# Spreading the delta-rule gate rows of a hybrid backbone by one bf16 product of three exact parts

## The chip, the cores and the metric

The kernel runs on 1 core of one Trainium2 chip. The metric is the time of one execution in device microseconds, as the median of several runs. Engines are named as in the profile: PE is TensorE (PEld its weight loads), DVE is VectorE, ACT is ScalarE, POOL is GpSimd, SP is SyncE, which issues most DMAs.

## The reference

A two-layer latent backbone with 256 latent tokens and 256 context tokens of width 1024. Layer 0 mixes by gated linear attention and Mamba-2, layer 1 by a conformer convolution and a bidirectional gated delta rule; a mixture of 16 experts follows each. The change touches the gates of the delta rule in layer 1 alone:

```
ga, gb, q, k, v, og, a_raw, b_raw = split_cols(h @ w_in + b_in, CD_SPLITS)
beta = sigmoid(b_raw)                                   # 2 directions x 8 heads
logg = -exp(gdn_a_log) * softplus(a_raw + gdn_dt_bias)  # 2 directions x 8 heads
# per chunk of 64 tokens and head:
gc = cumsum(logg)
decay = exp(where(tril, gc[:, None] - gc[None, :], -inf))
m = eye + where(strict, (k * beta) @ k.T * decay, 0)
u, w = solve(m, [v * beta, k * beta * exp(gc)])
aqk = (q @ k.T) * decay;   qg = q * exp(gc);   kd = k * exp(glast - gc)
```

So each head and direction needs its row of cumulative logs `gc` once along the partitions (a column per token) and once along the free axis, in every partition (a "spread" row), to form the differences of `decay`. The backward direction runs over the reversed sequence.

## The kernel before

Everything lives in SBUF, tokens on the free axis (T = 512: context first, then latent) or on 128 partitions in 4 tiles. The program is written out by hand for five engines; each works its queue in order and the order around the change is that of the code, tied by named semaphores.

**Projection of layer 1** (`project`, PE L804, ACT L1705, DVE L2273). The 49 column tiles of the input projection run over j. PE does the tile's 8 products (L820) and, two tiles behind, `turn` (L764), which transposes the convolved tile j-2. A q, k or v tile goes: PE tile j, ACT copy out of the bank (L1717), DVE's three-tap convolution at j (`convolve`, L2267, L2269, L2271), ACT's Silu (L1648), PE's `turn` in step j+2, DVE's copy out of the bank (`turned`, L2256). `turn` number m waits for its Silu and for the copy of turn m-2. Between these DVE runs the conformer's 31 taps a tile (L2280) and, at the end of a step j, a piece of the gate work (`gate_softplus(j)`, DVE L2315, ACT L1740).

**Gates.** Projection tile 0 ("small") holds the gate rows: the a columns (for the logs) of the two directions on partitions 0 to 7 and 32 to 39, the b columns (for beta) on 64 and 96 upward. DVE adds the bias at j = 2 (L2339), works out the softplus at j = 8 and 14 (L2715 to L2729), multiplies by -exp(a_log) (L2346), and at j = 16 takes the two cumulative sums (L2349, L2350) into `gcb`, which is the tile `small`. At j = 20 it lays the last values of each chunk on diagonals (`albuf2`, L2358). PE turns `gcb` to tokens-on-partitions and adds up `albuf2` at j = 24 (`gdn_gates`, L991, L992). DVE copies these out at j = 25 (L2323 to L2328), and PE waits for that before a modulation product at j = 28 (L627).

**The delta-rule scan** (`gdn`, PE L994, ACT L1769, DVE L2377, POOL L3088). Ten rounds `it` = -1 to 8; in a round head n = it+1 is prepared, head p = it is solved by six levels of block products (`level_r` L1013, `level_p` L1036) and head s = it-1 runs its state recurrence (`new_values` L1115, `state_step` L1127, `state_out` L1146). `spread(n, d)` (L1053) makes the spread row of head n and direction d: a column of the fp32 identity, broadcast to 128 columns, times `gcb` (128x512). There are 16 of them: d = 0 stands between `level_r(p, 1)` and `level_p(p, 1)`, d = 1 between `level_p(p, 1)` and `level_r(p, 2)`. ACT's `decay` (L1804 Abs, L1805 and L1807 Exp) reads the bank.

Of the kernel before, what the change touches and what calls it, by code (L numbers as in the profile page):

```python
# [12 lines left out]
P = 128  # L13
# [128 lines left out]
def hybrid_backbone(nc, A, out):  # L142
    rg = Ring()
    assert tuple(rg.place[rg.first[f"moe{layer}"]] % RING for layer in range(2)) == MOE_SLOT
    with ExitStack() as ctx:
# [112 lines left out]
        with ExitStack() as st:  # L258
# [6 lines left out]
            gts = sb("gts", [P, 7, NT, 2, 8], F32, st)  # L265
            alogx = sb("alogx", [P, 1], F32, st)
            rkq = sb("rkq", [P, KD, 6], F32, st)
# [13 lines left out]
            gcb = small[:, :]  # L281
            albuf2 = gts[:, 0:4, :, :, :].rearrange("p i t d h -> p i (t d h)")
            gcT, sT, negc, ekd, egl2, skT, ngcT = [gts[:, i, :, :, :] for i in range(7)]
# [318 lines left out]
        def _(pe):  # L602
# [384 lines left out]
            def gdn_gates():  # L987
                pe.wait_ge(sg("gate_cums"), 2)
                pe.wait_ge(sg("mod_added"), 5)
                for t in range(NT):  # L990
                    nc.tensor.transpose(ps[7][:, t * P:(t + 1) * P], gcb[:, t * P:(t + 1) * P], ident[:, :])  # L991
                mm(ps[6][:, 0:256], ones[:, :], albuf2, start=True, stop=True).then_inc(sg("gate_cums_turned"), 1)  # L992

            def gdn():  # L994
# [49 lines left out]
                def spread(n, d):  # L1044

                    if n >= KD:
                        return
                    if n > 0:
                        if d == 0:
                            pe.wait_ge(sg("gdn_S"), 2 * n)  # L1050
                        else:
                            pe.wait_ge(sg("gdn_aqk"), n)
                    mm(ps[4 + d], ident[:, n + 32 * d:n + 32 * d + 1].broadcast_to([P, P]), gcb,  # L1053
                       start=True, stop=True).then_inc(sg("gdn_spr"), 1)
# [519 lines left out]
        def _(act):  # L1574
# [165 lines left out]
            def gate_softplus(j):  # L1740
# [15 lines left out]
                if j == 1:  # L1756
                    act.drain()
                    A_(small[64:128, :], small[64:128, :], ACT.Sigmoid)
                if j == 3:
                    A_(small[64:128, :], small[64:128, :], ACT.Sqrt)  # L1760
                if j == 6:
                    act.wait_ge(sg("sp_abs"), 2)
                    A_(alogx[0:64, :], cols[0:64, COL_AT["gdn_alog"]:COL_AT["gdn_alog"] + 1], ACT.Exp)
                    A_(g_u[0:64, :], g_u[0:64, :], ACT.Exp, scale=-1.0).then_inc(sg("sp_u"), 1)
                if j == 12:
                    act.wait_ge(sg("sp_w"), 2)
                    A_(g_l[0:64, :], g_w[0:64, :], ACT.Ln).then_inc(sg("sp_ln"), 1)

# [338 lines left out]
        def _(dve):  # L2107
# [207 lines left out]
            def gate_softplus(j):  # L2315

                rows = slice(0, 64)
                if j - 2 in CD_HALVES and CD_HALVES[j - 2][1] == 1:
                    modulation(1, CD_HALVES[j - 2][0])
                if j == 25:  # L2320
                    dve.wait_ge(sg("gate_cums_turned"), 2)
                    tm = ps[7].rearrange("p (t d r) -> p t d r", t=NT, d=4)
                    V.tensor_copy(gcT, tm[:, :, 0:2, 0:8])  # L2323
                    V.tensor_scalar(ngcT, tm[:, :, 0:2, 0:8], -1.0, None, ALU.mult)
                    V.tensor_copy(sT, tm[:, :, 2:4, 0:8])
                    V.tensor_copy(egl2, ps[6][:, 0:256].rearrange("p (t d r) -> p t d r", t=NT, d=2)[:, :, :, 0:8])
                    dve.drain()
# [6 lines left out]
                if j == 45:  # L2334
                    key_scales(slice(0, 6), 4)
                    dve.drain().then_inc(sg("conf_ready"), 1)
                if j == 2:
                    dve.wait_ge(sg("proj_evacuated"), PLAN["cd"][0]["no"] + 1)
                    V.tensor_scalar(g_z[rows], small[rows, :], cols[rows, COL_AT["gdn_dtb"]:COL_AT["gdn_dtb"] + 1], None, ALU.add)  # L2339
# [4 lines left out]
                if j == 14:  # L2344
                    softplus_end(rows, g_z, g_u, g_l, g_sp)
                    V.tensor_scalar(small[rows, :], g_sp[rows], alogx[rows, :], -1.0, ALU.mult, ALU.mult)  # L2346
                if j == 16:
                    dve.drain()
                    V.tensor_tensor_scan(gcb[0:32, :], rst128[0:32, :], small[0:32, :], 0.0, ALU.mult, ALU.add)  # L2349
                    V.tensor_tensor_scan(gcb[32:64, ::-1], rst128[32:64, :], small[32:64, ::-1], 0.0, ALU.mult, ALU.add)  # L2350
                if j == 20:
# [3 lines left out]
                    for t in range(NT):  # L2355
                        for d in range(2):
                            e = t * P + edge(d)
                            last = V.tensor_scalar(albuf2[0:64, t, 32 * d:32 * d + 32], ident[0:64, 32 * d:32 * d + 32], gcb[0:64, e:e + 1], None, ALU.mult)  # L2358
                    last.then_inc(sg("gate_cums"), 1)
# [817 lines left out]
def pack_columns(np, a):  # L3177
# [31 lines left out]
    for d in range(2):  # L3209
        got[64 + 32 * d:80 + 32 * d, COL_AT["ssd_dtb"]] = a["ssd_dt_bias"][0, d]  # L3210
        got[64 + 32 * d:80 + 32 * d, COL_AT["ssd_alog"]] = a["ssd_a_log"][0, d]
        got[32 * d:32 * d + 8, COL_AT["gdn_dtb"]] = a["gdn_dt_bias"][0, d]
        got[32 * d:32 * d + 8, COL_AT["gdn_alog"]] = a["gdn_a_log"][0, d]
    b = a["cd_b_in"][0]
# [17 lines left out]
CD_PLACE = {"ga": 0, "gb": 1024, "q": 2048, "k": 3072, "v": 4096, "og": 5120}  # L3232
CD_SMALL = [(0, 6144, 8), (32, 6152, 8), (64, 6160, 8), (96, 6168, 8)]

# [69 lines left out]
```

## Time and profile before

| | |
|---|---|
| median of 3 runs | 2189.32 us (2188.63 to 2191.02) |
| span of the profiled execution | 2185.7 us; its time is not listed apart from the three runs', and the span is 3.6 us under their median |
| PE / DVE / ACT / POOL busy | 1882.4 / 804.4 / 507.6 / 335.2 us |
| projection of layer 1 | about 1142 to 1406 us of the span |
| delta-rule scan | about 1406 to 1661 us |
| output projection and second expert stage | 1661 us to the end; DMA engines 92% busy |
| the 16 spreads (L1053) | 32 PE records of 593 ns (an fp32 product leaves two records) |

Times in a timeline are microseconds from the span's start. "Busy" of PE is the time in which any product is in its pipeline, so neighbouring products overlap. Idle before an instruction stands in square brackets with what ended it. In the chain of waits a row is the part of an instruction that lies on the chain of work that ended last.

### The profile page before, as it was taken

Reading aid. Unit: us, or ns where it says so; the run is one execution under the profiler, and the core shown is the slowest. Engines: PE = TensorE matmul, PEld = TensorE weight load, DVE = VectorE, ACT = ScalarE, POOL = GpSimd, SP = SyncE. Lnnn points to the kernel's source line nnn. Section 1 sums busy time; section 2 is a strip of 40 time slices with the busy share of each in tenths; the row PEclk is TensorE's granted clock in tenths of the full one; section 3 lists DMA queues with packets and bytes.
Section 4 is the critical chain, followed back from the end, with each engine's and each line's share of the span. In section 5 each row is a group of like instructions: output and inputs, shape, how many; then the busy total and the mean of one; then the engine's idle time right before and its main releaser. Section 6 shows DMA issues by size and latency. Waiting matters only on the chain.

```text
span 2185.7 us, 32921 instructions
## 1 busy us (share of the span) xinstructions
PE 1882.4 (86%) x14024; PEld 1132.1 (52%) x14024; DVE 804.4 (37%) x1427; ACT 507.6 (23%) x1119; POOL 335.2 (15%) x323
## 2 busy tenths in 40 slices
PE   6999889999999998888889999989999975666565
PEld 3874668745875433333236556677787731212112
DVE  3331757555633010000026877566774300000001
ACT  2452321343012100001023323444442100000001
POOL 1431054322320000000013000054540000000000
PEclk9999999999999999999999999999999998878888
DMA  9321031240239999999993433200004699999997
GB/s 385 142 86 73 5 118 78 119 190 1 89 150 384 428 430 426 429 431 431 428 407 147 169 154 140 103 2 2 2 2 174 233 428 429 430 427 432 430 430 298
DMA packets 46689, 528.07 MB, mean 242 GB/s; under 512 B 3408, under 2 KB 7760, under 8 KB 23120
## 3 DMA queue, kind: packets, MB, share of 16 engines
q1 hardware_dynamic: 44784, 522.56, 57.3%
q10 hardware_dynamic: 1760, 3.42, 0.4%
q8 instruction: 111, 1.82, 0.3%
q14 instruction: 34, 0.28, 0.0%
HBM read 524.91 MB, written 1.05 MB: 241 GB/s over the span
## 4 chain that ended last, share of the span: by engine, by line
PE 53%; DMA 28%; DVE 12%; issue 2%; ACT 2%; DVEq 1%; PEld 1%; PEldq 0%; POOLq 0%; POOL 0%; ACTq 0%; SPq 0%
DMA ring<-in_moe_w 27%; PE bank L1435 12%; PE bank L709 8%; PE bank L820 7%; PE bank L1317 4%; PE bank L1250 3%; PE bank L788 3%; DVE ring L2421 2%; DVE x L2280 2%; PE bank L1036 2%; PE bank L1013 2%; DVE x L2859 1%; PE bank L961 1%; DMA ring<-in_mod_w 1%; PE bank L627 1%
## 5 line engine op out<-in xcount | busy, mean ns | idle before, releaser
L1435 PE MATMUL bank<-ring,xgs 128*32 128x512 f32 x2984 | 374.0, 655 | 129.4 <-DMA ring<-in_moe_w 128.0
L1435 PEld LDWEIGHTS bank<-ring,xgs 128*32 128x32 f32 x2984 | 106.3, 119 | 370.6 <-issue 284.9
L1435 PE MATMUL bank<-ring,hT 128*32 128x512 f32 x1488 | 190.1, 663 | 75.3 <-DMA ring<-in_moe_w 75.1
L820 PE MATMUL bank<-hT,ring 128*128 128x256 f32 (+1 forms) x784 | 232.7, 454 | 2.0 <-ACT hT L1607 1.4
L2700 DVE SCALAR_TENSOR_TENSOR x<-bank,modT,x 128x256 f32<-128x256 f32 x96 | 42.4, 480 | 457.1 <-PE bank L1461 456.9
L820 PEld LDWEIGHTS bank<-hT,ring 128*128 128x128 f32 x784 | 146.6, 190 | 82.3 <-issue 66.8
L1435 PEld LDWEIGHTS bank<-ring,hT 128*32 128x32 f32 x1488 | 52.3, 120 | 199.3 <-issue 152.6
L2280 DVE SCALAR_TENSOR_TENSOR x<-gluR,cols,x 128x256 f32<-128x256 f32 x240 | 116.2, 484 | 16.6 <-issue 0.9
L709 PE MATMUL bank<-hT,ring 128*128 128x256 f32 x432 | 99.9, 381 | 3.7 <-ACT ssd_g L1658 2.2
L709 PEld LDWEIGHTS bank<-hT,ring 128*128 128x128 f32 x432 | 81.1, 190 | 17.9 <-issue 6.2
L3091 POOL MEMSET gluR<- 128x3008 f32 x1 | 2.6, 2610 | 498.9 <-DVEq L2710 498.9
L2689 DVE TENSOR_TENSOR hT<-mrow,bank 128x512 f32<-128x512 f32 x16 | 11.0, 685 | 170.8 <-PE bank L1435 170.8
L2689 DVE TENSOR_TENSOR hT<-small,bank 128x512 f32<-128x512 f32 x8 | 5.5, 688 | 174.4 <-PE bank L1435 174.4
L3108 POOL TENSOR_TENSOR ring<-ring,pmask 128x512 f32<-128x512 f32 x40 | 51.0, 1274 | 77.8 <-DVE ring L2409 68.6
L1923 ACT ACTIVATE xgs<-bank 128x512 f32<-128x512 f32 x24 | 14.3, 597 | 197.0 <-PE bank L1392 197.0
L709 PE MATMUL bank<-g_v,ring 128*128 128x256 f32 x256 | 58.4, 381 | 0.0
L788 PE MATMUL bank<-ring,hT 128*128 128x512 f32 x128 | 55.2, 593 | 0.3 <-issue 0.3
L2961 POOL TENSOR_TENSOR ring<-ring 128x512 f32<-128x512 f32 x18 | 31.2, 1734 | 155.4 <-PE bank L709 155.4
L1392 PEld LDWEIGHTS bank<-pick,htok 128*128 128x128 f32 x384 | 44.5, 191 | 18.4 <-issue 17.2
L709 PEld LDWEIGHTS bank<-g_v,ring 128*128 128x128 f32 x256 | 47.9, 190 | 11.3 <-issue 4.0
L627 PE MATMUL bank<-ring,act_c 128*32 128x512 f32 x384 | 46.8, 635 | 7.6 <-DMA ring<-in_mod_w 5.3
L1933 ACT ACTIVATE mrow<-bank 128x512 f32<-128x512 f32 x16 | 9.5, 594 | 186.9 <-PE bank L1435 186.9
(573 smaller groups left out, 3026.0 us busy)
## 6 DMA issues: line engine op xcount, KB each, us to landing
ring<-in_moe_w SPq DMA_DIRECT2D x56, 4096.0 KB, 22.8
ring<-in_moe_w SPq DMA_DIRECT2D x28, 2048.0 KB, 21.1
ring<-in_moe_w SPq DMA_DIRECT2D x55, 1024.0 KB, 14.4
ring<-in_mod_w SPq DMA_DIRECT2D x12, 4096.0 KB, 13.4
ring<-in_moe_w SPq DMA_DIRECT2D x12, 3072.0 KB, 22.0
ring<-in_cd_w SPq DMA_DIRECT2D x6, 4096.0 KB, 14.1
ring<-in_ab_w SPq DMA_DIRECT2D x5, 4096.0 KB, 15.3
ring<-in_ab_wo SPq DMA_DIRECT2D x2, 4096.0 KB, 14.9
```

Source lines behind the costliest of these rows:

```text
L627: last = mm(ps[6][32 * g:32 * g + 32, :], act_c[:, 4 * kh + k, :], w[:, g, k, :], start=(kh == 0 and k == 0), stop=(kh == 1 and k == 3), t ...
L709: last = mm(to, w[:, k0 + k, :], right(k), start=(start and k == 0), stop=(k == 3), skip_group_check=True)
L788: last = mm(ps[n % 4].rearrange("p (e c) -> p e c", c=P), hT[:, k, t * P:t * P + P], w[:, e0:e0 + 4, k, :], start=(k == 0), stop=(k == KD ...
L820: last = mm(ps[p["no"] % 4][:, p["c0"]:T], w[:, k, :], hT[:, k, p["c0"]:T], start=(k == 0), stop=(k == KD - 1))
L1013: last = mm(U4[r, d ^ hf, t, :], S[r, d, t, r], H[r, d ^ hf, t, :], start=True, stop=True, skip_group_check=True, tile_position=(64 * hf, ...
L1036: last = mm(P4[r, v, t, :], H[r, v, t, :], Rs[r, v, t, :], start=True, stop=True, skip_group_check=True, tile_position=(64 * hf, 64 * hf))
L1250: last = mm(ps[c % 4][:, SEQ:T], w[:, k, :], conf[:, k, :] if k < 8 else og[:, k - 8, :], start=(k == 0), stop=(k == 15))
L1317: last = mm(out_banks(v)[bank], w[:, k0 + k, :], right[k], start=(start and k == 0), stop=(k == 7), skip_group_check=True)
L1392: last = mm(ps[(4, 7)[b % 2]][:, k * P:(k + 1) * P], htok[:, 2 * s + tt, ch:ch + P], pick[:, s, tt, P * q:P * q + P], start=(tt == 0), sto ...
L1435: last = mm(ps[banks + s][32 * j:32 * j + 32, :], lhs[s][:, 4 * kh + k, 32 * j:32 * j + 32], piece(g, k, j), start=(kh == 0 and k == 0), s ...
L2280: V.scalar_tensor_tensor(y, gluR[:, i, :, w:w + GW], col("conf_w", 8 * w + i), y, ALU.mult, ALU.add)
L3108: G.tensor_tensor(Hb[(l + 1) % 3], Fb[p % 2], pmask[:, l - 1, :].unsqueeze(1).unsqueeze(1).broadcast_to([P, 2, NT, 64]), ALU.mult).then_in ...
```

## The change

The a columns of the small tile are laid out three times: packed as 16 rows (direction, head) on partitions 0 to 15, 32 to 47 and 64 to 79, and the b columns on 96 to 111. All gate steps up to the logs run over 96 partitions instead of 64 (same number of columns). Each of the 96 rows gets both cumulative sums, of which a 0 or 1 column for its direction (`sides2`) has cleared the wrong one, and their sum is `gcb`. At j = 18 the fp32 row is cut into three bf16 parts, one in each group of partitions (`gcs`, in the storage of `rst128`), whose sum is the fp32 value. `pickb2` is a bf16 tile with three ones a column, so that one bf16 product picks a row and adds its three parts. `albuf2` shrinks from 64 to 16 columns a tile, and its product from 256 to 64 columns.

```
             gts = sb("gts", [P, 7, NT, 2, 8], F32, st)
-            alogx = sb("alogx", [P, 1], F32, st)
+            steps2 = sb("steps2", [P, 3], F32, st)
+            alogx, sides2 = steps2[:, 0:1], steps2[:, 1:3]
+            pickb2 = sb("pickb2", [P, 16], BF16, st)
...
-            albuf2 = gts[:, 0:4, :, :, :].rearrange("p i t d h -> p i (t d h)")
+            albuf2 = gts[:, 0, :, :, :].rearrange("p t d h -> p t (d h)")
+            gcs = rst128[:, :].bitcast(BF16)[:, 0:T]
...
-                mm(ps[6][:, 0:256], ones[:, :], albuf2, start=True, stop=True).then_inc(sg("gate_cums_turned"), 1)
+                mm(ps[6][:, 0:16 * NT], ones[:, :], albuf2, start=True, stop=True).then_inc(sg("gate_cums_turned"), 1)
...
-                    mm(ps[4 + d], ident[:, n + 32 * d:n + 32 * d + 1].broadcast_to([P, P]), gcb,
+                    mm(ps[4 + d], pickb2[:, 8 * d + n:8 * d + n + 1].broadcast_to([P, P]), gcs,
                        start=True, stop=True).then_inc(sg("gdn_spr"), 1)
...
-                    A_(small[64:128, :], small[64:128, :], ACT.Sigmoid)
+                    A_(small[96:128, :], small[96:128, :], ACT.Sigmoid)
...
-                rows = slice(0, 64)
+                rows = slice(0, 96)
...
                 if j == 2:
+                    V.tensor_tensor(pickb2[:, :], ident[:, 0:16], ident[:, 32:48], ALU.add)
+                    dve.drain()
+                    V.tensor_tensor(pickb2[:, :], pickb2[:, :], ident[:, 64:80], ALU.add)
+                    dve.drain()
+                    V.tensor_reduce(sides2, pickb2[:, :].rearrange("p (d h) -> p d h", d=2), AX.X, ALU.add)
                     dve.wait_ge(sg("proj_evacuated"), PLAN["cd"][0]["no"] + 1)
...
                     softplus_end(rows, g_z, g_u, g_l, g_sp)
-                    V.tensor_scalar(small[rows, :], g_sp[rows], alogx[rows, :], -1.0, ALU.mult, ALU.mult)
+                    V.tensor_scalar(sides2[rows, :], sides2[rows, :], alogx[rows, :], -1.0, ALU.mult, ALU.mult)
+                    dve.drain()
+                    V.tensor_scalar(g_w[rows], g_sp[rows], sides2[rows, 0:1], None, ALU.mult)
+                    V.tensor_scalar(g_l[rows], g_sp[rows], sides2[rows, 1:2], None, ALU.mult)
                 if j == 16:
                     dve.drain()
-                    V.tensor_tensor_scan(gcb[0:32, :], rst128[0:32, :], small[0:32, :], 0.0, ALU.mult, ALU.add)
-                    V.tensor_tensor_scan(gcb[32:64, ::-1], rst128[32:64, :], small[32:64, ::-1], 0.0, ALU.mult, ALU.add)
+                    V.tensor_tensor_scan(g_u[rows], rst128[rows, :], g_w[rows], 0.0, ALU.mult, ALU.add)
+                    V.tensor_tensor_scan(g_z[rows, ::-1], rst128[rows, :], g_l[rows, ::-1], 0.0, ALU.mult, ALU.add)
+                    dve.drain()
+                    V.tensor_tensor(gcb[rows, :], g_u[rows], g_z[rows], ALU.add)
+                if j == 18:
+                    dve.drain()
+                    V.tensor_copy(gcs, gcb)
+                    dve.drain()
+                    V.tensor_tensor(g_w[32:64, :], gcb[32:64, :], gcs[32:64, :], ALU.subtract)
+                    V.tensor_tensor(g_w[64:96, :], gcb[64:96, :], gcs[64:96, :], ALU.subtract)
+                    dve.drain()
+                    V.tensor_copy(gcs[32:64, :], g_w[32:64, :])
+                    V.tensor_copy(gcs[64:96, :], g_w[64:96, :])
+                    dve.drain()
+                    V.tensor_tensor(gcs[64:96, :], g_w[64:96, :], gcs[64:96, :], ALU.subtract)
                 if j == 20:
...
-                            last = V.tensor_scalar(albuf2[0:64, t, 32 * d:32 * d + 32], ident[0:64, 32 * d:32 * d + 32], gcb[0:64, e:e + 1], None, ALU.mult)
+                            last = V.tensor_scalar(albuf2[0:32, t, 8 * d:8 * d + 8], ident[0:32, 8 * d:8 * d + 8], gcb[0:32, e:e + 1], None, ALU.mult)
...
-CD_SMALL = [(0, 6144, 8), (32, 6152, 8), (64, 6160, 8), (96, 6168, 8)]
+CD_SMALL = [(32 * q + 8 * d, 6144 + 8 * d, 8) for q in range(3) for d in range(2)] + [(96, 6160, 8), (104, 6168, 8)]
```

The order of PE, ACT, POOL and SP stays as it was; only names and shapes of their rows change. DVE's queue gets twelve rows more, all in the projection of layer 1. The first place is step j = 2, DVE's queue before the change:

```order
L2280 SCALAR_TENSOR_TENSOR x<-gluR,cols,x 128x256 x6
L2339 TENSOR_SCALAR k_t<-small,cols 64x512
L2341 SCALAR_TENSOR_TENSOR v_t<-k_t 64x512
L2280 SCALAR_TENSOR_TENSOR x<-gluR,cols,x 128x256 x6
L2293 TENSOR_TENSOR gluR<-rstd,rst 128x4x64
```

and of the changed kernel, whose line numbers are a few higher:

```order
L2283 SCALAR_TENSOR_TENSOR x<-gluR,cols,x 128x256 x6
L2341 TENSOR_TENSOR pickb<-ident 128x16
L2343 TENSOR_TENSOR pickb<-pickb,ident 128x16
L2345 TENSOR_REDUCE steps<-pickb 128x2
L2347 TENSOR_SCALAR k_t<-small,cols 96x512
L2349 SCALAR_TENSOR_TENSOR v_t<-k_t 96x512
L2283 SCALAR_TENSOR_TENSOR x<-gluR,cols,x 128x256 x6
```

Three small instructions now stand ahead of the bias. The second place is the end of step 18 and the convolution of tile 19 in DVE's queue (a q tile, 256 columns), before:

```order
L2280 SCALAR_TENSOR_TENSOR x<-gluR,cols,x 128x256 x6
L2267 TENSOR_SCALAR wk<-wk,cols 128x256
L2269 SCALAR_TENSOR_TENSOR wk<-wk,cols 128x256
L2271 SCALAR_TENSOR_TENSOR wk<-wk,cols 128x256
L2256 COPY k_t<-bank 128x512
```

and of the change:

```order
L2283 SCALAR_TENSOR_TENSOR x<-gluR,cols,x 128x256 x6
L2366 CAST rst<-small 128x512
L2368 TENSOR_TENSOR q_t<-small,rst 32x512
L2369 TENSOR_TENSOR q_t<-small,rst 32x512
L2371 CAST rst<-q_t 32x512
L2372 CAST rst<-q_t 32x512
L2374 TENSOR_TENSOR rst<-q_t,rst 32x512
L2270 TENSOR_SCALAR wk<-wk,cols 128x256
L2272 SCALAR_TENSOR_TENSOR wk<-wk,cols 128x256
L2274 SCALAR_TENSOR_TENSOR wk<-wk,cols 128x256
L2259 COPY k_t<-bank 128x512
```

Six instructions stand ahead of the convolution of tile 19 and of the copy that frees a bank. The third place is DVE's end of step 16 (ahead of the convolution of tile 17), of the change:

```order
L2360 SCALAR_TENSOR_TENSOR v_t<-rst,q_t 96x512
L2361 SCALAR_TENSOR_TENSOR k_t<-rst,v_t 96x512
L2363 TENSOR_TENSOR small<-v_t,k_t 96x512
L2270 TENSOR_SCALAR wk<-wk,cols 128x512
L2272 SCALAR_TENSOR_TENSOR wk<-wk,cols 128x512
```

where the third row is new behind the two cumulative sums.

## Rows read from the trace of the kernel before

**Rows 1.** Two stages: length, busy PE, PEld, DVE, ACT, POOL; clock, DMA share, GB/s.
```profile
1158.00:1226.00 68.00, 64.20 (x254) 40.76 (x252) 58.42 (x114) 23.82 (x42) 10.38 (x32) 1.00 0.32 124
...
1406.00:1661.00 255.00, 234.20 (x3672) 198.91 (x3671) 169.39 (x287) 116.91 (x305) 113.53 (x88) 0.99 0.03 13
```

**Rows 2.** Timeline of PE in the projection: start, length, instruction, idle before and releaser.
```profile
1226.36 0.41 PE L764 MATMUL bank<-ident,wk 128*128 128x128 f32 x2 [0.72 <-DVE k_t L2256]
...
1259.78 0.38 PE L764 MATMUL bank<-ident,wk 128*128 128x128 f32 x2
...
1270.75 0.63 PE L991 MATMUL bank<-ident,small 128*128 128x128 f32 x4 [0.26 <-issue]
...
1291.28 3.64 PE L627 MATMUL bank<-ring,act_c 128*32 128x512 f32 x32 [1.15 <-DVE gts L2328]
```

**Rows 3.** Timeline of DVE in the projection.
```profile
1225.53 0.68 DVE L2256 COPY k_t<-bank 128x512 f32<-128x512 f32 x1
...
1234.28 0.68 DVE L2729 SCALAR_TENSOR_TENSOR k_t<-k_t 64x512 f32<-64x512 f32 x1
1235.04 0.48 DVE L2346 TENSOR_SCALAR small<-k_t,alogx 64x512 f32<-64x512 f32 x1
...
1248.72 0.49 DVE L2267 TENSOR_SCALAR wk<-wk,cols 128x512 f32<-128x512 f32 x1 [0.37 <-ACTq L1719]
...
1255.62 0.68 DVE L2256 COPY k_t<-bank 128x512 f32<-128x512 f32 x1
...
1264.27 1.25 DVE L2358 TENSOR_SCALAR gts<-ident,small 64x32 f32<-64x32 f32 x8
...
1271.28 0.49 DVE L2267 TENSOR_SCALAR wk<-wk,cols 128x512 f32<-128x512 f32 x1 [1.21 <-ACTq L1719]
...
1279.47 0.49 DVE L2267 TENSOR_SCALAR wk<-wk,cols 128x512 f32<-128x512 f32 x1 [2.49 <-ACTq L1719]
```

**Rows 4.** DVE's groups by shape: count, busy us, mean ns, idle before.
```profile
L2721 DVE TENSOR_TENSOR k_t<-k_t,v_t 64x512 f32<-64x512 f32 x1 | 0.7, 684 | 0.1
L2715 DVE TENSOR_SCALAR q_t<-v_t 64x512 f32<-64x512 f32 x1 | 0.4, 419 | 0.1
L2369 DVE TENSOR_TENSOR gts<-gts,rkq 128x16 f32<-128x16 f32 x1 | 0.2, 170 | 0.0
```

**Rows 5.** The spreads of line 1053, and the bf16 products of layer 0.
```profile
L1053 PE MATMUL bank<-small,ident x32: 592/593/721, 1406.9 to 1593.6; 128*128 128x512 f32 x32
```
```profile
L921 PE MATMUL bank<-m_far,identb 128*128 128x512 bf16 x32 | 9.7, 384 | 0.0
```

**Rows 6.** The chain of waits, at step 24 and at the scan's start.
```profile
1271.38 0.43 PE bank L992 x2
...
1406.91 1.14 PE bank L1053 x2
```

**Rows 7.** The chain of waits in the round of head 3.
```profile
1504.36 1.68 DVE ring L2421
...
1508.54 0.65 DVE ring L2409
```

**Rows 8.** Timeline of ACT at the scan's start and of PE in head 3's round.
```profile
1408.14 1.14 ACT L1804 ACTIVATE gluR<-bank,gts 128x128 f32<-128x128 f32 x4 [2.41 <-PE bank L1053]
...
1504.49 1.02 PE L1053 MATMUL bank<-small,ident 128*128 128x512 f32 x2
1505.44 1.15 PE L1036 MATMUL bank<-ring 64*64 64x64 f32 x32
...
1509.23 1.15 PE L1013 MATMUL bank<-ring,hT 64*64 64x64 f32 x32 [1.14 <-DVE ring L2409]
```

**Rows 9.** Three stretches of the scan, columns as in the first group.
```profile
1439.00:1443.00 4.00, 2.46 (x52) 2.05 (x46) 3.40 (x4) 0.65 (x2) 1.77 (x2) 1.00 0.00 2
1443.00:1447.00 4.00, 3.73 (x38) 3.12 (x38) 3.92 (x4) 2.04 (x3) 3.08 (x3) 0.57 0.00 0
1505.00:1509.00 4.00, 3.09 (x40) 1.75 (x38) 3.97 (x6) 2.36 (x8) 1.71 (x2) 1.00 0.02 4
```

**Rows 10.** The block product of line 1013 at the lowered clock.
```profile
1443.27 1.98 PE L1013 MATMUL bank<-ring,hT 64*64 64x64 f32 x32 [0.28 <-DVE ring L2421]
```

More of the change, by code:

```diff
@@ L1757, in gate_softplus @@
                     act.drain()
-                    A_(small[64:128, :], small[64:128, :], ACT.Sigmoid)
+                    A_(small[96:128, :], small[96:128, :], ACT.Sigmoid)
                 if j == 3:
-                    A_(small[64:128, :], small[64:128, :], ACT.Sqrt)
+                    A_(small[96:128, :], small[96:128, :], ACT.Sqrt)
                 if j == 6:
                     act.wait_ge(sg("sp_abs"), 2)
-                    A_(alogx[0:64, :], cols[0:64, COL_AT["gdn_alog"]:COL_AT["gdn_alog"] + 1], ACT.Exp)
-                    A_(g_u[0:64, :], g_u[0:64, :], ACT.Exp, scale=-1.0).then_inc(sg("sp_u"), 1)
+                    A_(alogx[0:96, :], cols[0:96, COL_AT["gdn_alog"]:COL_AT["gdn_alog"] + 1], ACT.Exp)
+                    A_(g_u[0:96, :], g_u[0:96, :], ACT.Exp, scale=-1.0).then_inc(sg("sp_u"), 1)
                 if j == 12:
                     act.wait_ge(sg("sp_w"), 2)
-                    A_(g_l[0:64, :], g_w[0:64, :], ACT.Ln).then_inc(sg("sp_ln"), 1)
+                    A_(g_l[0:96, :], g_w[0:96, :], ACT.Ln).then_inc(sg("sp_ln"), 1)
             def gdn():
@@ L2321, in gate_softplus @@
                     dve.wait_ge(sg("gate_cums_turned"), 2)
[L2322 to L2326, printed above, removed]
+                    tm = ps[7].rearrange("p (t d r) -> p t d r", t=NT, d=16)
+                    V.tensor_copy(gcT, tm[:, :, 0:2, :])
+                    V.tensor_scalar(ngcT, tm[:, :, 0:2, :], -1.0, None, ALU.mult)
+                    V.tensor_copy(sT, tm[:, :, 12:14, :])
+                    V.tensor_copy(egl2, ps[6][:, 0:16 * NT].rearrange("p (t d r) -> p t d r", t=NT, d=2))
                     dve.drain()
@@ L3211, in pack_columns @@
         got[64 + 32 * d:80 + 32 * d, COL_AT["ssd_alog"]] = a["ssd_a_log"][0, d]
-        got[32 * d:32 * d + 8, COL_AT["gdn_dtb"]] = a["gdn_dt_bias"][0, d]
-        got[32 * d:32 * d + 8, COL_AT["gdn_alog"]] = a["gdn_a_log"][0, d]
+        for q in range(3):
+            got[32 * q + 8 * d:32 * q + 8 * d + 8, COL_AT["gdn_dtb"]] = a["gdn_dt_bias"][0, d]
+            got[32 * q + 8 * d:32 * q + 8 * d + 8, COL_AT["gdn_alog"]] = a["gdn_a_log"][0, d]
     b = a["cd_b_in"][0]
```

## The prediction

> **What bounds the kernel now.** I read the time by stages first, then the chain of waits stage by stage, then the timelines around each line that the change touches. The change has two places. Most of its DVE work falls into the projection of layer 1, its 16 cheaper products into the scan. In both stages PE is busy nearly all the time, 64.2 of 68 us and 234.2 of 255 us [rows 1], and in both DVE, busy for less, is what PE waits for at the few places where it waits. In the projection DVE starts late, works without a pause from 1158 us, and PE waits for it at the turn of tile 13 (0.72 us at 1226.36) and for the gate columns at 1291.28 (1.15 us) [rows 2]. Between these PE goes at its own pace, and what DVE gains or loses there is seen only at the turns. In the scan each head's round has a part in which DVE is on the chain, from first_level (L2421) to the masked copy at 1508.54 [rows 7], and a part in which PE is. The spreads stand in DVE's part.
>
> **The spreads, removed cost.** A spread is now two fp32 records of 593 ns [rows 5], together 1.02 us from the first's start to the second's end [rows 8]. The bf16 products of layer 0 with the same 512 columns leave one record of 384 ns [rows 5]. So each spread gets shorter by 1.02 - 0.38 = 0.64 us, and 16 of them by 10.2 us of PE time. Where is that on the path? In the round of head 3, the first spread runs at 1504.49, level_p behind it ends at 1505.44 + 1.15 = 1506.59 [rows 8], and DVE takes that product only at about 1508.5, when it has finished its own row of work [rows 7]. That is 1.9 us of slack for level_p before the change. Behind the second spread PE sits idle for 1.14 us until DVE's copy lets L1013 start at 1509.23 [rows 8]. Both savings end in waits for DVE, and the chain of waits has no L1053 in this round. ACT's decay begins 0.64 us earlier and then waits for the same level 2. The other rounds have the same pattern, and the two odd ones (first heads) are bound there by DVE's copies or by ACT's tables. I take nothing for 15 spreads. The first spread is different: it is on the chain for 1.14 us [rows 6], and ACT has waited 2.41 us for it when it starts at 1408.14 [rows 8]. With one record of 0.38 us in the place of 1.14 us this saves 0.76 us, and the second spread of that head is not waited for, since ACT is busy with the first. Bounds: 0.5 to 1.0 us saved there, and 0 to 15 x 0.64 = 9.6 us more if the slack isn't real (a rival below).
>
> **The product of line 992.** It shrinks from 256 to 64 columns; of its 0.43 us on the chain [rows 6] a quarter stays, so 0.3 us less of PE, in a stretch in which PE is the bound.
>
> **DVE's added work, by step.** Instructions behind a drain start 0.08 us after the one before has ended (1234.28 + 0.68 to 1235.04) [rows 3].
> - j = 2: two TENSOR_TENSOR of 128x16 and a small reduce. The row of that shape is 170 ns [rows 4]; with the drains 3 x 0.25 = 0.75 us. Bounds 0.4 to 1.1.
> - j = 14: a 96x2 multiply, 0.25 us, and two scaled copies for one; the one took 0.48 [rows 3], the second adds 0.40. Together 0.65 us. Bounds 0.4 to 0.9.
> - j = 16: the sums cost by columns, not by partitions, so only the added TENSOR_TENSOR counts: 0.68 [rows 4] + 0.08 = 0.76 us. More partitions cost nothing at j = 2, 8 and 14 for the same reason: a TENSOR_SCALAR of 64x512 takes 0.48 and of 128x512 0.49 [rows 3].
> - j = 18: three TENSOR_TENSOR of 512 columns, 3 x 0.68 [rows 4] = 2.04, and three casts to bf16. No cast is in the trace. A one-source instruction from SBUF to SBUF takes 0.42 [rows 4], a copy out of PSUM 0.68 [rows 3]; I take 0.42, since source and target lie in SBUF as there. With 1.26 for the casts and about 0.24 for the drains less the overlap of undrained neighbours, 3.54 us. Bounds 2.4 (casts at half) to 4.6 (casts and joins slower).
> - j = 20: eight multiplies of 8 columns for 32, up to 0.5 us less of 1.25 [rows 3], and a smaller memset. I take 0.3 less.
>
> For the casts the Trainium skill (VectorE: DVE Perf Modes, the perf-mode tier table) says that one-source instructions with both ends in SBUF move two fp32 elements a cycle, and that two-source ones and PSUM operands in fp32 drop to one. The trace agrees: 419 ns against 684 and 683 ns for 512 columns [rows 3, 4]. By the rule a cast is like the 0.42; by the copy's row the three casts would cost 0.8 us more and the sum below would end at 2191.0.
>
> **What hides it.** I follow DVE's lag against the rows of before. Behind j = 2, 14 and 16 it is 0.75 + 0.65 + 0.76 = 2.16 us. The convolution of tile 18 waited 0.37 us for ACT at 1248.72 [rows 3], so 1.8 us remain. Steps 17 and 18 of PE have their Silu more than that ahead. Then comes j = 18, straight in front of the convolution of tile 19: the lag is 1.8 + 3.54 = 5.33 us. The turn of tile 19 needs that convolution, its Silu and the copy of turn 17, which ended at 1255.62 + 0.68 = 1256.30; with the 0.15 us that lay between such a copy's end (1225.53 + 0.68) and the product at 1226.36, PE could have started at 1256.45 and did so at 1259.78 [rows 2, 3]. Slack 3.33 us. So **PE waits and ends up 5.33 - 3.33 = 2.0 us late**. The 0.75 us from j = 2 show first, at the turns up to 1226.36, and are part of these 2.0.
>
> Is more lost later? At the gates' turn (1270.75 before [rows 2]) PE comes at 1272.8; DVE's diagonals, ended at 1265.5, end at about 1270.5. No wait. At tile 23 DVE had waited 1.21 us and at tile 24 2.49 us for ACT [rows 3]. Lag 5.0 at tile 23 becomes 5.0 - 1.21 = 3.8, less 2.49 leaves 1.3, while PE and ACT are 2.0 - 0.3 = 1.7 us late. So from tile 24 DVE waits for ACT again, with some 0.4 us to spare, and the wait for the gate columns at 1291.28 stays 1.15 us. Everything behind, with the scan and the experts' weight stream that starts on its last output, is shifted by the same amount.
>
> **Sum.** +2.0 (turn of tile 19) - 0.3 (L992) - 0.76 (first spread) = +0.9 us. The span goes from 2185.7 to 2186.6. The span lies 3.6 us under the median of 2189.32; with this unchanged, **2190.2 us**. With all bounds on DVE's work low, the cost is 0.1 instead of 2.0; with all high (lag 2.9 - 0.37 + 4.6 = 7.1), 3.8. So the likeliest case runs from 2188.0 to 2192.3.
>
> **Rivals.**
> - *The spreads are on the path after all (faster).* If in each round PE's or ACT's time around the spreads counted, 15 x 0.64 = 9.6 us would come on top: 2180.6 us. For it: PE is busy 92% of the scan [rows 1]. Against it: the chain of each full round passes from L2421 by DVE to L1013, and PE idles right behind the second spread [rows 7, 8].
> - *TensorE's clock falls in the scan (slower).* The products taken away also kept PE busy. In the first head's round a stretch of 4 us with PE busy for 2.46 was followed by 4 us at a granted clock of 0.57, between its levels of 1.2 and 2.4 GHz [rows 9], and the block product then took 1.98 us instead of 1.15 [rows 8, 10]. In the round of head 3, 1505 to 1509 us had PE busy 3.09 us at full clock [rows 9]; without the 1.28 us of two spreads it is 1.8, less than what went ahead of the fall. Right behind stands PE's part of the round, so a fall costs in full: about two such blocks, 2 x 0.83 = 1.7 us a round, over 7 rounds 11.6 us, 2201.8 us. If it happens in half of the rounds, 2196. It decides over 0.2% from three falls on. Against it: 1505 to 1509 lost 0.91 us of PE to idling already, and the clock stood; the one fall came in the one round where the block products also had pauses between them.
> - *DVE's small instructions and drains cost twice as much (slower).* The lag at tile 24 isn't absorbed, and the wait at 1291.28 grows beside the one at 1259.78: lag 8 us gives +4.7 at the turn of tile 19, 2193 to 2194.
> - *The bf16 product isn't shorter.* Then only the 0.76 us are missing, 2191.0. The layer-0 rows speak against it; it is inside the likeliest case.
>
> On the clock the Trainium skill (TensorE: Matmul & The Clock Gate, on the failure mode of PSUM-queue cycling) reports a kernel with short idles between groups of matmuls whose clock swings between both levels. That speaks against this change, as the second rival has it; the trace before shows one such swing in the scan and none in the rounds behind.
>
> **Chances.** Likeliest case 0.70, spreads on the path 0.09, the clock 0.15, DVE twice as dear 0.06. A measurement of this kernel tells about 0.2%, 4.4 us, from no change. Faster by more: 0.09 and 0.01 from noise in the likeliest, 0.10. Slower by more: 0.13 of the clock's 0.15 and 0.04 of DVE's 0.06, 0.17. Within: 0.73. The range takes the likeliest case whole and half of the clock's and most of DVE's: 2186 to 2196.5.
>
> **What would show it.** L1053 with 16 records of about 384 ns. PE idle ahead of the turn of tile 19 by about 1.2 to 2 us, released by DVE, and 1.15 us still ahead of the product at j = 28. Casts of 0.42 us. In the scan rounds as long as before, with PE idle ahead of L1013 at about 1.8 us instead of 1.14, and first ACT decay 1.2 - 0.76 = 0.5 us behind the spread's start. The forecast is wrong if the round gets shorter (first rival), or if the granted clock leaves 1.0 in rounds where it was 1.0 (second).

## The result: 6 us slower, and the profile after

| | before | changed |
|---|---|---|
| median of 8 runs each | 2188.98 us (2187.64 to 2193.13) | 2195.15 us (2192.88 to 2200.08) |
| span of the profiled execution | 2185.7 us | 2192.2 us (that execution: 2193.93 us) |

The ratio is 1.0028 (95% interval 1.0019 to 1.0036): slower by 0.28%, 6.2 us, inside the stated range but above the likeliest case, which ended at 2192.3. In the experiments below, one of the 12 runs of experiment 9 took 3216.04 us at a granted clock of 0.56 over the whole execution, and its ratio leaves this run out. The page of the changed kernel shows no more work than was counted; PE, DVE and ACT are busy for about as long as before. Its clock line, in tenths, reads 9 over the scan's slices as before; the change is too short-lived for it:

```profile
span 2192.2 us, 32909 instructions
PE 1885.1 (86%) x14008; PEld 1135.1 (52%) x14008; DVE 809.4 (37%) x1439; ACT 507.1 (23%) x1119; POOL 335.2 (15%) x323
PEclk9999999999999999999999999999999997878888
```

The two stages that the change touches, changed kernel (columns as in [rows 1]):

```profile
1158.00:1226.00 68.00, 63.38 (x250) 40.06 (x249) 58.49 (x116) 23.88 (x42) 9.87 (x30) 1.00 0.32 124
1406.00:1661.00 255.00, 226.99 (x3626) 197.73 (x3625) 167.09 (x278) 115.73 (x302) 113.91 (x90) 0.96 0.04 14
```

In the scan's window the granted clock is 0.96 where it was 0.99 [rows 1].

**The projection** did what the sum said. PE's timeline of the changed kernel:

```profile
1226.24 0.41 PE L767 MATMUL bank<-ident,wk 128*128 128x128 f32 x2 [0.73 <-DVE k_t L2259]
...
1260.55 0.41 PE L767 MATMUL bank<-ident,wk 128*128 128x128 f32 x2 [0.73 <-DVE k_t L2259]
1271.55 0.63 PE L994 MATMUL bank<-ident,small 128*128 128x128 f32 x4 [0.26 <-issue]
1291.87 3.64 PE L630 MATMUL bank<-ring,act_c 128*32 128x512 f32 x32 [1.15 <-DVE gts L2331]
```

The second row is the turn of tile 19. It had no wait before [rows 2] and now waits for DVE's copy, 0.73 us, on top of what earlier turns passed on. At 1291.87 the wait is 1.15 us as before. DVE's timeline has the instructions that cause it:

```profile
1161.68 0.17 DVE L2341 TENSOR_TENSOR pickb<-ident 128x16 bf16<-128x16 f32 x1
1161.93 0.17 DVE L2343 TENSOR_TENSOR pickb<-pickb,ident 128x16 bf16<-128x16 bf16 x1
1162.18 0.17 DVE L2345 TENSOR_REDUCE steps<-pickb 128x2 f32<-128x16 bf16 x1
1162.27 0.54 DVE L2347 TENSOR_SCALAR k_t<-small,cols 96x512 f32<-96x512 f32 x1
...
1254.76 0.43 DVE L2366 CAST rst<-small 128x512 bf16<-128x512 f32 x1
1255.26 0.68 DVE L2368 TENSOR_TENSOR q_t<-small,rst 32x512 f32<-32x512 f32 x1
...
1258.33 0.35 DVE L2270 TENSOR_SCALAR wk<-wk,cols 128x256 f32<-128x256 f32 x1
...
1280.06 0.49 DVE L2270 TENSOR_SCALAR wk<-wk,cols 128x512 f32<-128x512 f32 x1 [0.33 <-ACTq L1722]
```

The split takes 1258.33 - 1254.76 = 3.6 us, and at tile 24 DVE waits for ACT again (0.33 us left of 2.49 [rows 3]).

**The spread** is one record, 389 ns at the median, and the first ACT decay waits 1.68 us where it waited 2.41 [rows 8]:

```profile
L1056 PE MATMUL bank<-rst,pickb x16: 379/389/634, 1407.5 to 1596.7; 128*128 128x512 bf16 x16
```
```profile
1408.00 1.14 ACT L1807 ACTIVATE gluR<-bank,gts 128x128 f32<-128x128 f32 x4 [1.68 <-PE bank L1056]
```

**The scan's rounds** are where the rest went. PE's timeline in head 3's round:

```profile
1507.83 0.39 PE L1056 MATMUL bank<-rst,pickb 128*128 128x512 bf16 x1 [0.23 <-DVE gluR L2463]
1510.24 1.54 PE L1016 MATMUL bank<-ring,hT 64*64 64x64 f32 x32 [2.02 <-DVE ring L2433]
1511.71 1.22 PE L1149 MATMUL bank<-ring,hT 128*128 128x128 f32 x4
1512.86 1.75 PE L1039 MATMUL bank<-ring 64*64 64x64 f32 x32
```

PE is idle for 0.23 us ahead of the second spread, where it did not wait before, and for 2.02 us ahead of the level's products instead of 1.14 [rows 8], and then these products are slow: 1.54 and 1.75 us in place of 1.15. The windows of the same kernel give the granted clock (last three columns: clock, DMA share, GB/s):

```profile
1442.00:1454.00 12.00, 9.80 (x126) 7.99 (x125) 9.90 (x12) 7.04 (x15) 6.56 (x6) 0.57 0.00 1
1506.00:1510.00 4.00, 1.99 (x37) 1.43 (x33) 3.97 (x6) 2.26 (x8) 1.72 (x2) 1.00 0.02 6
1510.00:1516.00 6.00, 5.76 (x88) 5.18 (x90) 4.38 (x9) 3.15 (x9) 2.46 (x2) 0.72 0.00 0
1540.00:1546.00 6.00, 5.69 (x86) 5.12 (x88) 4.46 (x9) 3.15 (x9) 2.56 (x3) 0.72 0.01 3
1598.00:1604.00 6.00, 4.91 (x73) 4.50 (x74) 4.37 (x9) 2.53 (x7) 2.45 (x2) 0.72 0.01 3
```

A stretch with the clock at its lower level is called a fall from here on. The first lasts some 10 us of 1442 to 1454 (a mean of 0.57 of a clock that is either 1.0 or 0.5); three more of some 3.4 us each stand right behind the idle time of three rounds, in the windows from 1510, 1540 and 1598. The second window is the part of head 3's round that 1505 to 1509 was before, since this round starts 1.0 us later. PE is busy for 1.99 us of its 4, where it was for 3.09 [rows 9]; the forecast's second rival had 1.8. But neither this nor the idle time decides alone: the round of head 5 has as much of both and no fall.

```profile
1566.15:1570.15 4.00, 1.98 (x37) 1.43 (x33) 3.97 (x6) 2.25 (x8) 1.73 (x2) 1.00 0.01 4
```
```profile
1570.39 1.15 PE L1016 MATMUL bank<-ring,hT 64*64 64x64 f32 x32 [2.03 <-DVE ring L2433]
```

The chain of waits carries the slow products of head 3's round in full:

```profile
1509.48 0.72 DVE ring L2433
1510.24 1.54 PE bank L1016 x32
1511.78 1.15 PE bank L1149 x4
1512.93 1.68 PE bank L1039 x32
```

A balance by landmarks that both timelines have (first tile of the projection; last turn; first product of L1086; each round's start of L1017; first product of L1250; end). The round of head n is the one in which head n is solved; it holds the two spreads of head n+1, and head 7's holds none:

| stretch | before | changed | difference |
|---|---|---|---|
| start to first tile of the projection | 1142.52 | 1141.69 | -0.8 (nothing changed there) |
| projection, first tile to last turn | 262.65 | 264.08 | +1.4 |
| last turn to first product of L1086 | 9.96 | 9.22 | -0.7 |
| first product of L1086 to the first round | 25.24 | 25.23 | 0 |
| first round (head 1) | 30.37 | 31.50 | +1.1 |
| the six that follow (heads 2 to 7) | 29.07, 28.69 x4, 26.12 | 29.08, 30.08, 30.08, 28.70, 30.07, 26.11 | +4.2 |
| last round | 22.67 | 22.68 | 0 |
| output projection and experts | 522.35 | 523.68 | +1.3 |

Of the six rounds the three with a fall (heads 3, 4 and 6) are 1.38 to 1.39 us longer each, and the others are as before. Scan together: +4.6 us.

### The profile page after: what moved, and what is told of

Read it like the earlier page. It is cut to its first block, busy times and chain, and to the rows that moved or that the text cites. A ratio compares the mean times of both kernels' runs of the same rounds, so it can differ in the third digit from the quotient of the medians.

```text
span 2192.2 us, 32909 instructions
## 1 busy us (share of the span) xinstructions
PE 1885.1 (86%) x14008; PEld 1135.1 (52%) x14008; DVE 809.4 (37%) x1439; ACT 507.1 (23%) x1119; POOL 335.2 (15%) x323
## 4 chain that ended last, share of the span: by engine, by line
PE 52%; DMA 27%; DVE 13%; issue 2%; ACT 2%; DVEq 2%; PEld 0%; PEldq 0%; POOLq 0%; POOL 0%; ACTq 0%; SPq 0%
DMA ring<-in_moe_w 26%; PE bank L1438 13%; PE bank L712 8%; PE bank L823 6%; PE bank L1320 3%; PE bank L1253 3%; PE bank L791 3%; DVE x L2283 2%; DVE ring L2445 2%; PE bank L1039 2%; PE bank L1016 2%; DMA ring<-in_mod_w 1%; DVE x L2883 1%; PE bank L964 1%; PE bank L1395 1%
## 5 line engine op out<-in xcount | busy, mean ns | idle before, releaser
L1438 PE MATMUL bank<-ring,hT 128*32 128x512 f32 x1488 | 195.0, 678 | 69.3 <-DMA ring<-in_moe_w 69.3
```

Source lines behind the costliest of these rows:

```text
L1438: last = mm(ps[banks + s][32 * j:32 * j + 32, :], lhs[s][:, 4 * kh + k, 32 * j:32 * j + 32], piece(g, k, j), start=(kh == 0 and k == 0), s ...
```

## Experiments

The theory after the first look (clock theory): the products taken away had kept TensorE's clock up; it now falls right behind the idle time in front of a PE-bound stretch. The rival: DVE's new work, or something it shifts, costs all of it. In each experiment the ratio is against the kernel before, run beside it on the same chip: 2190.03 us for experiments 1 to 4, 2188.88 for 5 to 7, 2190.03 for 8 and 9, on three chips. Windows and rounds are read from one profiled execution of each version. An idle product is one whose result nobody uses. "Rounds" means the start-to-start times of line 1017's product as in the table.

**1. Only the spread's product undone.**

```
-mm(ps[4 + d], pickb2[:, 8 * d + n:8 * d + n + 1].broadcast_to([P, P]), gcs,
+mm(ps[4 + d], ident[:, n + 8 * d:n + 8 * d + 1].broadcast_to([P, P]), gcb,
```

> The changed kernel with the 16 spreads made by the fp32 product again (a column of the fp32 identity times the fp32 rows); all of DVE's new work stays, and nobody uses the bf16 parts. Clock theory (TensorE's clock falls in the scan because the shorter spreads leave it idle for longer): the granted clock leaves 1.0 in the scan once, as in the kernel before, the falls at heads 3, 4 and 6 (1.4 us each) are gone, only the 1.4 us of the projection stay: about 1.4 us over before, 2190.4. Rival (DVE's new work costs the rest, somewhere behind the projection): as the changed kernel, about 6 us over before, 2195. Noise rival (the 6 us are a slow expert stage): anything between, with the scan as long as in the changed kernel's trace.

Measured 2190.99 us (2188.27 to 2193.35), before 2190.03; ratio 1.0005 (0.9996 to 1.0014). The projection takes 264.07 us, as in the changed kernel, and rounds 30.36, 29.08, 28.70, 28.71, 28.72, 28.73, 26.10 us, as before. The windows of the places of the falls:

```profile
1442.00:1454.00 12.00, 7.26 (x138) 5.85 (x139) 9.88 (x11) 5.66 (x15) 5.79 (x4) 1.00 0.01 1
1512.00:1518.00 6.00, 5.17 (x109) 4.61 (x110) 4.84 (x10) 3.08 (x10) 3.20 (x3) 1.00 0.00 1
1600.00:1606.00 6.00, 5.94 (x117) 5.28 (x116) 3.59 (x7) 4.71 (x12) 4.61 (x5) 1.00 0.01 3
```

With all of DVE's new work in place there is no fall in the scan at all. The DVE rival is gone for 5 of the 6 us. There is a second finding: the first round takes 30.36 us with the clock at 1.00, and took 30.37 before with 4 us at 0.57 [rows 9]. So the one fall of before cost nothing.

**2. The bf16 product kept, its lost PE time put back by idle products.**

```
+if n > 0:
+    for _ in range(3):
+        mm(ps[4 + d][:, 0:P], ident[:, :], ident[:, :], start=True, stop=True, skip_group_check=True)
 mm(ps[4 + d], pickb2[:, 8 * d + n:8 * d + n + 1].broadcast_to([P, P]), gcs,
```

> The changed kernel with three extra fp32 128x128 products, results unused, ahead of each of the 14 spreads of heads 1 to 7, in the spread's own bank: 0.66 us of PE's time for the 0.64 us that the bf16 product took out. Clock theory: at most one fall in the scan, 4 to 5 us faster than the changed kernel, about 0.7 to 1 us over before. Rival (the falls come from something else, as DVE's or ACT's shifted work): falls as in the changed kernel and its time, 2195, or more if the extra products cost.

Measured 2190.82 us (2187.56 to 2194.3); ratio 1.0006 (0.9997 to 1.0015). The rounds of heads 2 to 7 are as before (29.10, 28.70 to 28.72 and 26.14 us), the idle time ahead of the level's products is 1.09 us, and no fall is left in them; one is left in the first round, head 1's:

```profile
1444.00:1456.00 12.00, 11.16 (x133) 9.72 (x133) 9.86 (x12) 6.70 (x14) 6.55 (x6) 0.57 0.01 1
1511.00:1517.00 6.00, 4.85 (x87) 3.97 (x86) 5.65 (x11) 3.19 (x10) 2.50 (x3) 1.00 0.02 4
```

It lasts some 10 us there instead of 3.4 and makes that round 32.17 us. The median is 0.8 us over before where the changed kernel was 6.2.

**3. Only the bf16 product, nothing of DVE's work ahead of tile 19.**

```
+gcs = rst128[:, :].bitcast(BF16)[:, 0:T]
...
+if j == 36:
+    V.tensor_copy(gcs, gcb)
...
-mm(ps[4 + d], ident[:, n + 32 * d:n + 32 * d + 1].broadcast_to([P, P]), gcb,
+mm(ps[4 + d], identb[:, n + 32 * d:n + 32 * d + 1].broadcast_to([P, P]), gcs,
```

> The kernel before with one bf16 cast of the cumulative logs at step 36, where DVE has slack, and the bf16 spread of it; the two smaller parts of the split are left out, so the decays have bf16 precision only. Nothing is added to DVE ahead of the turn of tile 19. Clock theory: projection as before (no wait at the turn of tile 19), 0.75 us saved at the first spread, but the clock falls in 2 to 4 rounds at 1.4 us each and the first fall is longer: 2 to 5 us over before, 2191 to 2194. Rival (only DVE's work makes it slower): 0.75 us faster than before, 2188.2.

Measured 2195.08 us (2192.21 to 2199.31); ratio 1.0024 (1.0015 to 1.0033). The projection is the old one (262.68 us), the first spread saves its 0.7 us, and the clock falls five times, three of them in the rounds of heads 2, 4 and 5, of 30.45, 30.05 and 30.10 us. Two windows of it, and the turn of tile 19 without a wait:

```profile
1484.00:1490.00 6.00, 6.00 (x104) 5.42 (x102) 3.84 (x8) 3.16 (x9) 3.27 (x3) 0.72 0.01 3
1542.00:1548.00 6.00, 5.46 (x78) 4.89 (x80) 4.37 (x9) 2.95 (x9) 2.45 (x2) 0.72 0.01 3
```
```profile
1262.07 0.38 PE L765 MATMUL bank<-ident,wk 128*128 128x128 f32 x2
```

The faster product alone, with no wait added to the projection, makes the kernel 5.1 us slower, most of the whole change's 6.2 and more than the 2 to 5 expected.

**4. DVE's work moved, product as changed.** The three small instructions go from step 2 to step 0, where DVE is idle, and the split goes from step 18 to step 36.

```
-                if j == 2:
+                if j == 0:
                     V.tensor_tensor(pickb2[:, :], ident[:, 0:16], ident[:, 32:48], ALU.add)
...
-                if j == 18:
+                if j == 36:
```

> The changed kernel with the three small DVE instructions of step 2 moved to step 0, where DVE is idle, and the split of step 18 moved to step 36; PE as in the changed kernel. Projection: the lag ahead of tile 19 is 1.5 us against 3.3 us of slack, so no wait there, 1.4 us faster in the projection than the changed kernel (and 0.3 us less than before by the smaller product). Clock theory: the falls in the scan stay, total 4 to 5 us over before, 2193.5. DVE rival: all of the 6 us gone, 2188.

Measured 2195.86 us (2193.62 to 2199.52); ratio 1.003 (1.002 to 1.004). The projection takes 262.62 us: the 1.4 us are gone. But the total did not move; this profile (of an execution of 2198.58 us, 2.7 over the median) has seven falls and a scan of 264.95 us (first product of L1250 less last turn), against 262.75 in the changed kernel. Expected were 4 to 5 us over before, measured 5.8. Two of the falls lie ahead of the first round, where the changed kernel's profile had none:

```profile
1416.00:1422.00 6.00, 5.03 (x30) 4.39 (x28) 0.76 (x2) 4.99 (x17) 2.54 (x2) 0.72 0.14 56
1430.00:1436.00 6.00, 5.18 (x82) 4.40 (x82) 1.34 (x2) 3.43 (x9) 3.81 (x4) 0.72 0.00 0
```

The smaller product of L992 should have made the projection 0.3 us shorter than before. It isn't, because step 36 is not free of cost either; PE waits 0.80 us for DVE at a turn behind it, where it sat idle for 0.26 in the changed kernel:

```profile
1362.04 0.41 PE L767 MATMUL bank<-ident,wk 128*128 128x128 f32 x2 [0.80 <-DVE k_t L2259]
```

**5. Both remedies**: work moved, three idle products ahead of each spread.

> The moved DVE work and three extra 128x128 fp32 products ahead of each spread of heads 1 to 7, together. Clock theory: at most one fall in the scan; projection as before; first spread 0.75 us shorter: 0.5 to 1 us under before, no difference by the measurement. 5 to 6 us under the moved version alone. If the moved split at step 36 itself makes the clock fall or delays something (rival), it stays at 2193 or over.

Measured 2187.72 us (2185.62 to 2192.48), before 2188.88; ratio 0.9997 (0.9988 to 1.0006). Projection 262.64 us, scan 257.64 us against 258.18 before, rounds as before, the first with a fall of some 3.4 us. Counted from before, that is 7 us less than experiment 4, by 42 idle products; 5 to 6 were expected.

**6. More of them in one place.** Eight ahead of the second spread of heads 1 to 7, none ahead of the first (`if n > 0 and d == 1:`, `range(8)`).

> The moved DVE work and eight extra products (1.8 us of PE) ahead of the second spread of heads 1 to 7 alone, none ahead of the first: the idle time of about 2.0 us ahead of line 1013's products is nearly filled. Clock theory, by idle time: no fall in the rounds of heads 1 to 7; at or up to 1.5 us under before, as good as three ahead of each or better. If the extra products delay line 1013's (rival: the idle time was not free), 7 x 0.2 us or more is lost.

Measured 2192.08 us (2190.19 to 2195.62); ratio 1.0014 (1.0006 to 1.0023). The rounds of heads 2 to 7 are as before, with 0.36 us of idle time left ahead of the level's products, so there the idle time was free. No fall in the first round either was expected, and that was wrong: this round takes 33.34 us, with the clock low for most of 1446 to 1458:

```profile
1446.00:1458.00 12.00, 9.33 (x103) 8.47 (x103) 9.74 (x12) 6.69 (x14) 6.55 (x6) 0.57 0.01 1
1514.00:1520.00 6.00, 5.58 (x92) 4.92 (x94) 5.65 (x11) 2.82 (x9) 2.53 (x3) 1.00 0.02 4
```
```profile
1455.48 2.51 PE L1058 MATMUL bank<-ident 128*128 128x128 f32 x16
1458.14 1.15 PE L1016 MATMUL bank<-ring,hT 64*64 64x64 f32 x32
```

The eight products of this round, of two records each, take 2.51 us here, and the level's products follow with no idle time ahead of them. So in this one round the added products stand in PE's way, as the rival had it.

**7. A third of the time put back**: one product ahead of each spread.

> The moved DVE work and one extra product (0.22 us) ahead of each spread of heads 1 to 7: a third of the PE time that the bf16 product took out. Clock theory: falls rarer than without fill but not gone, 2 to 4 of them; between the versions with no fill (about 5 us over before) and with three (at before): 1 to 4 us over before. If any product in that place were enough, it would equal the version with three.

Measured 2192.91 us (2191.64 to 2197.15); ratio 1.0021 (1.0013 to 1.003). Falls in the same three rounds as in the changed kernel (30.09, 30.08, 30.09 us), behind an idle time of 1.72 us:

```profile
1509.94 1.34 PE L1016 MATMUL bank<-ring,hT 64*64 64x64 f32 x32 [1.72 <-DVE ring L2437]
```

One product is not enough to remove any of them; the dose matters.

**8. The fill by round**: three ahead of both spreads of heads 1 and 2, eight ahead of the second spread of heads 3 to 7 (`if n > 0 and (d == 1 or n < 3)`, `range(8 if n >= 3 else 3)`).

> The moved DVE work; three extra products ahead of both spreads of heads 1 and 2, and for heads 3 to 7 eight ahead of the second spread alone. If the eight-product version lost its 3 us because its first spreads of heads 1 and 2 had none (the fall in the first heads' round then lasted 10 us), this one is as the version with three ahead of each: first round 30.4 us, 0.5 to 1 us under before. If the eight products themselves cost, it stays about 3 us over before.

Measured 2188.71 us (2185.92 to 2190.57), before 2190.03; ratio 0.9993 (0.9985 to 1.0002). First round 30.41 us. So the loss of experiment 6 lay at the first two heads and not in the eight products of the later rounds. Whether it came from the products missing ahead of their first spreads, as expected, or from the eight ahead of their second isn't shown, since both were changed.

**9. Five ahead of each.**

> The moved DVE work and five extra products (1.1 us) ahead of each spread of heads 1 to 7, more PE time than before the change. Clock theory: as with three, no costly fall, at or 0.5 to 1 us under before. Line 1036's product is pushed back by 1.1 instead of 0.66 us, with 1.9 us of slack: no cost by that. Rival: the added products cost as soon as they exceed what was taken out, 2 to 3 us.

Measured 2190.06 us, before 2190.03; ratio 1.0001 (0.9992 to 1.001). No costly fall. The stretch from L1086 to the first round, 25.79 us, and the first round, 30.85 us, are 0.5 us longer each than in experiment 5. More than three doesn't help.

**10 and 11. The changed kernel and the kernel before once more.**

> The changed kernel once more, one look at where the clock falls. Clock theory: 2 to 5 falls in the scan, each round with one 1.4 us longer, not the same rounds as in the first profile if the phase of the monitor decides; the projection at 264.1 us again.

> The kernel before once more, one look. Clock theory: no fall in the rounds of heads 2 to 7, all of them 28.7 us; 0 or 1 fall in the first heads' round. If it has falls there too, the difference to the changed kernel is one of frequency, and single profiles say little.

The changed kernel: 2196.28 us, span 2194.4; projection 264.01; rounds 31.47, 29.08, 30.07, 30.10, 28.71, 30.08, 26.13. Its windows:

```profile
1512.00:1518.00 6.00, 5.63 (x84) 5.05 (x86) 4.37 (x9) 3.11 (x9) 2.45 (x2) 0.72 0.00 0
1542.00:1548.00 6.00, 5.53 (x80) 4.96 (x82) 4.58 (x9) 3.01 (x9) 2.46 (x2) 0.72 0.01 3
1600.00:1606.00 6.00, 4.74 (x72) 4.33 (x73) 4.38 (x9) 2.53 (x7) 2.46 (x2) 0.72 0.01 3
```

The kernel before: 2188.78 us, rounds 30.36, 29.07, 28.69, 28.68, 28.69, 28.71, 26.11, with one fall, in the first. I had held it possible that the changed kernel's falls come in other rounds than in the first profile; they are in the same three, heads 3, 4 and 6.

## Why the forecast's likeliest case was wrong and its second rival right

**Right, with small errors of size.** The spread's record: 384 ns forecast, 389 measured. DVE's split: 3.54 us forecast, 3.6 measured, with casts at 0.42 to 0.43 us. By the rule of the Trainium skill (VectorE: DVE Perf Modes, the perf-mode tier table) a cast was to be like the row of 0.42 us; the trace agrees, and the copy's row of 0.68 us was the wrong neighbour. The step at j = 2: 0.75 forecast, 1162.27 - 1161.68 = 0.6 measured, since the last small one overlaps what follows. The turn of tile 19: 2.0 us late forecast; counted from the first tile, 1260.55 - 1141.69 = 118.86 against 1259.78 - 1142.52 = 117.26, so 1.6. The product of L992 and the first spread: 0.3 and 0.76 forecast, 0.2 and 0.74 measured. That the wait at 1291 stays 1.15 us, and that DVE is free again at tile 24: both so, with 0.33 us to spare (0.4 forecast). These terms sum to +0.7 us, +0.9 forecast. (With the low bounds as listed, the turn's cost comes out as 0.3 us and not 0.1; nothing hangs on it.) Experiment 1 shows that what is left with fp32 spreads is about 1 us, experiment 4 that moving DVE's work takes the projection's 1.4 us away.

**Right: the other spreads save nothing.** No version has a round of heads 3 to 6 under 28.68 us, and the first rival is refuted. In head 3's round DVE's part, from the copies of L2421 (1502.69 before, 1503.69 in the changed kernel) to the level's products, takes 6.54 us before and 6.55 after. PE's idle time in it goes from 1.14 to 0.23 + 2.02 us, 1.1 more for the 1.28 that two spreads lost. The forecast's 1.8 us counted one spread of the two. Its "the other rounds have the same pattern" holds for heads 3 to 6; head 7's, which has no spreads, sits idle for only 0.17 us there, with or without the change.

**Wrong: "I take nothing for 15 spreads".** Their time was hidden, but it wasn't without a use. The forecast had this as its second rival at a chance of 0.15 and took the granted clock of 1.0 in the rounds of before as evidence that it would stay. It was at an edge, as the profiles of the versions show:

| version | PE idle ahead of the level's products, heads 3 to 6 | PE busy in the 4 us from 5.2 us behind the start of head 3's round | falls in heads 2 to 7 |
|---|---|---|---|
| before | 1.14 us | 3.09 us | none |
| changed kernel | 2.02 | 1.99 | 3, 4, 6 |
| experiments 3 and 4 | 2.02 | 1.99 | 2, 4, 5 |
| experiment 7, one product | 1.72 | 2.49 | 3, 4, 6 |
| experiments 2 and 5, three | 1.09 and 1.10 | 3.16 and 3.00 | none |
| experiment 6, eight | 0.36 | 3.65 | none |

A fall was to cost 1.7 us a round and costs 1.38. That half of the rounds was to give 2196 and 2195.15 was measured is in part luck: the three falls are 4.2 us, and the other 2 come from the terms above, the first round (+1.1) and the last stage (+1.3, open), less 0.8 at the start. The stated range held the measured time only because it took in half of this rival. Both arguments against it failed. That 0.91 us of idling left the clock at 1.0 said nothing of 2 us. And pauses between block products were not needed: head 3's round fell without one.

The row to weigh was not the clock of before but PE's idle time directly ahead of a PE-bound stretch, 1.14 us [rows 8], which the change was bound to lengthen. The Trainium skill (TensorE: Matmul & The Clock Gate, on the failure mode of psum-queue depth-cycling) reports of another kernel that short idle times between groups of products made the clock swing between its levels; the trace of the changed kernel agrees, in three of the five rounds of heads 2 to 6, with idle times of 2.02 to 2.40 us.

**Open.** Why the falls come in heads 3, 4 and 6 and not in 2 and 5, twice in the same rounds and in experiment 7 too, while experiments 3 and 4 have them in heads 2, 4 and 5. The length of the idle time isn't the reason: it is 2.02 or 2.03 us in each of heads 3 to 6, and head 2's of 2.40 us had no fall in the changed kernel. Mere chance is unlikely, since both profiles of the changed kernel agree. Where in time a round lies could matter; no run varies it by itself. Why the fall of the first round lasts some 10 us in some profiles and 3.4 in others: the added products alone don't set it, for experiments 2 and 5 have the same ones in the scan and differ in this. Whether idle products in bf16 would do the same: all were fp32. Each version but two has one profile; the medians of 11 or 12 runs are in keeping with them. The last stage's 1.3 us: it took 523.7 us in both profiles of the changed kernel and in experiment 6, and 522.2 to 522.7 us in all others; not explained.

**Against both kernels.** Experiments 5 and 8 measure 1.2 and 1.3 us under before, within what can't be told from no change (ratios 0.9997 and 0.9993). Against the changed kernel they gain some 7 us by the ratios. The three-part bf16 product brings no gain here that a measurement can tell.

## What to carry to other kernels

Where TensorE waits anyway and its work is made shorter, ask what the longer idle time does to its clock and where a fall would land. Here one of some 3.4 us in the first round cost nothing, and one over a stretch bound by TensorE cost 1.38 us. A round with TensorE on the chain behind an idle time of 1 to 2 us is a place to look at, even where the clock reads 1.0 now. If work leaves it, put idle products of the same duration back and compare, before anything else is blamed.

## What the runs showed of the hardware

- A fall (6 us at a mean granted clock of 0.72) made a round 1.4 us longer, in thirteen rounds over five profiles (30.05 to 30.10 us for 28.68 to 28.74), almost the same price each time.
- Little decides: with spreads of 0.39 us and one added 0.22 us product each (1.72 us idle), falls in three rounds; with three added products each (1.10 us idle), in none of the six rounds behind the first.
- A fall in the first round (4 us at a mean of 0.57) cost 0.01 us (30.37 us against 30.36 with none).
- fp32 to bf16 casts of 512 columns take 0.42 to 0.43 us on DVE, the same for 32 and 128 partitions, and a TENSOR_TENSOR of 512 columns 0.68 us with fp32 or mixed operands.
